# Sums over heads in a scan: squares as the moving operand, and spreading back by contractions over two rows

## The reference

```
kk = (k * k_k).reshape(b, L, 1, H, N)
kk = kk * rsqrt(sum(kk * kk, axis=-1, keepdims=True) + 1e-12)
... y = scan of both directions, summed ...
mean = mean(y, axis=-1, keepdims=True)
var = mean(square(y - mean), axis=-1, keepdims=True)
y = (y - mean) * rsqrt(var + GN_EPS) * ln_w + ln_b
bonus = sum(r * k_dir * r_k, axis=(2, 4))[..., None] * v
out = (y + bonus) * g
```

## Time and profile before

| | us |
|---|---|
| median of 3 runs | 2915.07 |
| lowest, highest | 2907.82, 2916.02 |
| the profiled execution | 2910.93 |
| its span | 2909.2 |
| PE busy | 2653.8 (91%) |
| PEld busy | 2209.6 (76%) |
| DVE busy | 1241.4 (43%) |
| ACT busy | 668.9 (23%) |
| POOL busy | 827.3 (28%) |

### The profile page before, as it was taken

How to read it: one execution, slowest core, us unless ns; L and a number is a source line. 1 busy time by engine, 2 the same in 40 slices (tenths; PEclk the granted TensorE clock), 3 DMA queues, 4 the chain that set the end, 5 groups by cost and what they waited for, 6 DMA issues and landing times. The chain is left out here.

```text
span 2909.2 us, 68114 instructions
## 1 busy us (share of the span) xinstructions
PE 2653.8 (91%) x29216; PEld 2209.6 (76%) x29216; DVE 1241.4 (43%) x2236; ACT 668.9 (23%) x1544; POOL 827.3 (28%) x644
## 2 busy tenths in 40 slices
PE   3987997997997999999999799596999999999997
PEld 2885456886886899998989655485888888888886
DVE  5003663551111444444444322565445544544545
ACT  3101551110001444444444211131011001101102
POOL 1222113332332233232333000543233233333324
PEclk9998998998998999999999999798999999999999
DMA  4111102101221000000000143432011111101113
GB/s 119 42 44 38 32 17 81 42 22 62 86 85 57 4 4 4 3 4 3 4 3 4 40 152 116 150 123 80 29 43 36 36 36 43 36 29 50 36 43 130
DMA packets 60191, 143.10 MB, mean 49 GB/s; under 512 B 12112, under 2 KB 31184, under 8 KB 59472
## 3 DMA queue, kind: packets, MB, share of 16 engines
q1 hardware_dynamic: 46176, 114.36, 12.0%
q10 hardware_dynamic: 10256, 12.49, 1.4%
q0 software_dynamic: 3552, 13.11, 1.1%
HBM read 108.48 MB, written 31.46 MB: 48 GB/s over the span
## 5 line engine op out<-in xcount | busy, mean ns | idle before, releaser
L1905 DVE TENSOR_TENSOR f<-f,ff_pd 128x512 f32<-128x512 f32 x320 | 214.2, 684 | 153.2 <-PE ff_pd L94 153.1
L1891 DVE TENSOR_TENSOR ff_sq<-ff_rl 128x512 f32<-128x512 f32 (+1 forms) x96 | 102.8, 1071 | 295.6 <-ACT ff_rl L1852 295.6
L1852 ACT ACTIVATE ff_rl<-ff_pu 128x512 f32<-128x512 f32 (+1 forms) x96 | 50.6, 527 | 759.0 <-PE ff_pu L94 759.0
L580 PE MATMUL sc_ps<-sc_xy,sc_q 64*64 64x64 f32 x3200 | 198.1, 221 | 0.0
L1053 DVE TENSOR_TENSOR sc_q<-sc_ps,sc_cs 128x128 f32<-128x128 f32 x400 | 113.6, 290 | 163.5 <-PE sc_ps L568 162.5
L577 PE MATMUL sc_ps<-sc_q,sc_xy 64*64 64x64 f32 x2560 | 170.6, 222 | 0.0
L568 PE MATMUL sc_ps<-sc_xy,sc_ai 64*64 64x64 f32 x3200 | 160.0, 223 | 1.4 <-ACT sc_xy L890 0.9
L890 ACT ACTIVATE sc_xy<-sc_ps 128x256 f32<-128x256 f32 x320 | 122.5, 383 | 160.3 <-PE sc_ps L580 159.7
L580 PEld LDWEIGHTS sc_ps<-sc_xy,sc_q 64*64 64x64 f32 x3200 | 156.1, 137 | 2.1 <-issue 1.0
L94 PE MATMUL ff_pu<-h2h,ff_wu0h 128*128 128x512 f32 (+1 forms) x384 | 136.8, 356 | 14.2 <-POOL ff_wu0l L1800 14.2
L429 POOL TENSOR_SCALAR sc_fac<-sc_icl,params,sc_k1a 128x512 f32<-128x512 f32 x20 | 15.3, 767 | 432.3 <-DVE sc_xy L955 414.5
(11 more groups left out here) (275 smaller groups left out, 7246.3 us busy)
## 6 DMA issues: line engine op xcount, KB each, us to landing
ff_wr<-in_w_up SPq DMA_DIRECT2D x32, 512.0 KB, 3.2
ff_wr<-in_w_down SPq DMA_DIRECT2D x32, 512.0 KB, 3.2
g_dram<-gp_g ACTq DMA_DIRECT2D x16, 640.0 KB, 2.9
mb_gate<-g_dram SPq DMA_DIRECT2D x8, 1280.0 KB, 8.9
gp_w<-in_w_in SPq DMA_DIRECT2D x16, 512.0 KB, 3.5
sp_w<-in_w_in SPq DMA_DIRECT2D x15, 512.0 KB, 3.5
n_x<-in_x SPq DMA_DIRECT2D x10, 512.0 KB, 3.6
m_dram<-mb_mo POOLq DMA_DIRECT2D x8, 640.0 KB, 8.9
```

The lines of the kernel that those rows point to most:

```text
L580: last = nc.tensor.matmul(y_out[g][rows, u, :], Q1[g][rows, u, :], XY[g][rows, 1, u, :], start=True, stop=True)
L1852: nc.scalar.activation(rl[u % 2][:, 0:tn], pu[b][:, 0:tn], ACT.Relu).then_inc(relu, 1)
L1891: nc.vector.tensor_tensor(sq[u % 2][:, 0:tn], rl[u % 2][:, 0:tn], rl[u % 2][:, 0:tn], ALU.mult).then_inc(squared, 1)
L1905: nc.vector.tensor_tensor(at, at, pd[d % 4][:, :], ALU.add).then_inc(added, 1)
```

## The change

- Two constants more: `by_heads`, 128x32, whose first two columns pick the channels of the two heads and whose other 30 are zero, and `by_row`, 128x128, which at rows 32p and 32p+1 (p = 0, 1, 2) has a one for each channel of the first or second head. The constants' load grows from 384 to 544 columns.
- `by_head` now has `by_heads` as weights and 512 tokens of the squares as moving operand, once for each of the three pieces, into partitions 32p to 32p+31 of one bank. The last piece takes the last 512 tokens, of which 256 are used.
- The square root and the inverse work on 96 partitions by 512 columns. The 1/64 of the variance is now the scale of the square root.
- `spread` and its POOL copies go, and with them two semaphores.
- `back` is one matmul for a piece: `by_row` at two rows as weights, the inverse norms at the same two rows as moving operand. Its wait is for the inverse.
- In front of the first step, the wait for the scan's constants moves ahead of `back`.

```diff
-        norms = [sb(f"sc_n{n}", [P, 2 * NT]) for n in range(2)]
+        norms = [sb(f"sc_n{n}", [P, 512]) for n in range(2)]
+        place = lambda p: slice(32 * p, 32 * p + 2)
+        full_piece = lambda p: slice(min(GROUPS[p][0], T - 512), min(GROUPS[p][0], T - 512) + 512)
+        in_piece = lambda p: slice(512 - GROUPS[p][1], 512)
+        placed = slice(0, 32 * NG)
...
-            def spread(ready, turn, norm, buf, done):
-                pool.wait_ge(ready, turn + 1)
-                nc.gpsimd.tensor_copy(buf[:, :].rearrange("p (n t) -> p n t", t=C),
-                                      norm[:, :].unsqueeze(2).to_broadcast([P, 2 * NT, C])).then_inc(done, 1)
...
-            def by_head(bank, sq, sums, done):
-                for n in range(NT):
-                    last = nc.tensor.matmul(ps[:, bank, 2 * n:2 * n + 2], sq[:, n * P:(n + 1) * P],
-                                            sums[:, 0:P:HD], start=True, stop=True)
-                last.then_inc(done, 1)
-
-            def back(bank, spread, p, done):
-                for m, n in enumerate(tiles_of(p)):
-                    last = nc.tensor.matmul(ps[:, bank, m * P:(m + 1) * P], spread[:, n * P:(n + 1) * P], ident,
+            def by_head(bank, sq, done):
+                for p in range(NG):
+                    last = nc.tensor.matmul(ps[32 * p:32 * p + 32, bank, :], by_heads, sq[:, full_piece(p)],
                                             start=True, stop=True)
                 last.then_inc(done, 1)
+
+            def back(bank, norm, p, done):
+                w = GROUPS[p][1]
+                nc.tensor.matmul(ps[:, bank, 0:w], by_row[place(p), :], norm[place(p), in_piece(p)], start=True, stop=True
+                                 ).then_inc(done, 1)
...
-                nc.scalar.activation(norms[1][:, :], ps[:, bank, 0:2 * NT], ACT.Sqrt,
-                                     bias=params[:, PM_EPS + 1:PM_EPS + 2]).then_inc(std_ready, 1)
+                nc.scalar.activation(norms[1][placed, :], ps[placed, bank, :], ACT.Sqrt, scale=1.0 / HD,
+                                     bias=params[placed, PM_EPS + 1:PM_EPS + 2]).then_inc(std_ready, 1)
...
-                nc.vector.reciprocal(norm[:, :], norm[:, :]).then_inc(done, 1)
+                nc.vector.reciprocal(norm[placed, :], norm[placed, :]).then_inc(done, 1)
...
-            pe.wait_ge(rnb_ready, 1)
+            pe.wait_ge(rn_ready, 1)
+            pe.wait_ge(cs_in, 16)
             for p in range(NG):
-                back(p, nrm, p, rnb_ps)
-            pe.wait_ge(cs_in, 16)
+                back(p, norms[0], p, rnb_ps)
```

More of the change, by code:

```diff
@@ L51 @@
 CN_ID, CN_ONES, CN_MEAN = 0, 128, 256
-CN_N = 384
+CN_HEADS, CN_ROWS = 384, 416
+CN_N = 544
 CS_G = BT
@@ L304, in _, with scan_mixer @@
             dve.wait_ge(shifted, E_SH + 2)
-def scan_mixer(nc, lora, params, cn_scan, ident, ones, mean, sT):
+def scan_mixer(nc, lora, params, cn_scan, ident, ones, mean, by_heads, by_row, sT):
     with ExitStack() as ctx:
@@ L363, in scan_mixer @@
             sem("p_ps"), sem("p"), sem("u_ps"), sem("u"), sem("s_ps"), sem("s"), sem("y_ps"), sem("y"))
[L364 to L367, removed]
+        sqk_ready, ss_ps, nrm_ready, rn_ready, rnb_ps, kk_ready = (
+            sem("sqk"), sem("ss_ps"), sem("nrm"), sem("rn"), sem("rnb_ps"), sem("kk"))
+        mean_ps, yc_ready, sqy_ready, var_ps, std_ready, rs_ready, rsb_ps, yn_ready = (
+            sem("mean_ps"), sem("yc"), sem("sqy"), sem("var_ps"), sem("std"), sem("rs"),
             sem("rsb_ps"), sem("yn"))
@@ L405, in turn_of @@
             return p if ct == CT - 1 else (0, 2, 1)[p]
-        def tiles_of(p):
-            return range(GROUPS[p][0] // P, (GROUPS[p][0] + GROUPS[p][1]) // P)
         @block.sync
@@ L480, in _ @@
             pool.wait_ge(scaled, 2)
-            spread(rn_ready, 0, norms[0], nrm, rnb_ready)
             prepare(0)
@@ L488, in _ @@
                     bonus_in(ct - 1)
[L489 to L492, removed]
                 if i == 3 and ct > 0:
@@ L672, in side @@
                     pe.wait_ge(sqy_ready, ct * NG)
-                    by_head(GRAM_BANK, std, mean, var_ps)
+                    by_head(GRAM_BANK, std, var_ps)
                 if i == 1 and ct + 1 < CT and l == 1:
@@ L676, in side @@
                     pe.wait_ge(sqk_ready, (ct + 2) * NG)
-                    by_head(TOK_BANK, nrm, ones, ss_ps)
+                    by_head(TOK_BANK, nrm, ss_ps)
                 if i == 1 and ct > 0 and l == 2:
@@ L686, in side @@
                     if p == 0:
-                        pe.wait_ge(rsb_ready, ct)
+                        pe.wait_ge(rs_ready, ct)
                     else:
                         pe.wait_ge(yn_ready, c * NG + 1)
-                    back(GRAM_BANK, std, p, rsb_ps)
+                    back(GRAM_BANK, norms[1], p, rsb_ps)
                 if i == 3 and ct + 1 < CT and p is not None:
                     if p == 0:
-                        pe.wait_ge(rnb_ready, ct + 2)
+                        pe.wait_ge(rn_ready, ct + 2)
                     else:
                         pe.wait_ge(kk_ready, (ct + 1) * NG + 1)
-                    back(GRAM_BANK, nrm, p, rnb_ps)
+                    back(GRAM_BANK, norms[0], p, rnb_ps)
                 if i == 4 and ct > 0 and p is not None:
@@ L712, in side_late @@
                 if i == 2 and ct > 0:
-                    back(TOK_BANK, std, 1, rsb_ps)
+                    back(TOK_BANK, norms[1], 1, rsb_ps)
                 if i == 3 and ct + 1 < CT:
-                    back(TOK_BANK, nrm, 1, rnb_ps)
+                    back(TOK_BANK, norms[0], 1, rnb_ps)
                 if i == 4 and ct > 0:
@@ L732, in _ @@
             pe.wait_ge(sqk_ready, NG)
-            by_head(GRAM_BANK, nrm, ones, ss_ps)
+            by_head(GRAM_BANK, nrm, ss_ps)
             lora_products(0, 0, 3)
             lora_products(0, 1, 3)
-            pe.wait_ge(rnb_ready, 1)
+            pe.wait_ge(rn_ready, 1)
+            pe.wait_ge(cs_in, 16)
             for p in range(NG):
-                back(p, nrm, p, rnb_ps)
-            pe.wait_ge(cs_in, 16)
+                back(p, norms[0], p, rnb_ps)
             pe.wait_ge(nrm_ready, 1)
@@ L806, in _ @@
             pe.wait_ge(sqy_ready, CT * NG)
-            by_head(STATE_BANK, std, mean, var_ps)
-            pe.wait_ge(rsb_ready, CT)
+            by_head(STATE_BANK, std, var_ps)
+            pe.wait_ge(rs_ready, CT)
             for p in range(NG):
-                back(p, std, p, rsb_ps)
+                back(p, norms[1], p, rsb_ps)
             pe.wait_ge(bv_ready, CT * NG)
@@ L1938, in encoder @@
         params, cn = sb("params", [P, PM_N]), sb("cn", [P, CN_N])
-        ident, ones, mean = (cn[:, c:c + P] for c in (CN_ID, CN_ONES, CN_MEAN))
+        ident, ones, mean, by_row = (cn[:, c:c + P] for c in (CN_ID, CN_ONES, CN_MEAN, CN_ROWS))
+        by_heads = cn[:, CN_HEADS:CN_HEADS + 32]
         with nc.semaphore("const_in") as const_in, nc.Block() as block:
@@ L1955, in encoder @@
                 gate_projection(nc, a["w_in"], params, H, g_dram)
-            scan_mixer(nc, a["lora"], params, a["cs"], ident, ones, mean, sT)
+            scan_mixer(nc, a["lora"], params, a["cs"], ident, ones, mean, by_heads, by_row, sT)
             merge_branches(nc, a["w_proj"], g_dram, oa_dram, sT[:, 0:CT, :], m_dram)
@@ L1970, in host_constants @@
     heads = np.kron(np.eye(2, dtype=np.float32), np.ones((HD, HD), np.float32))
-    cn = np.concatenate([eye, heads, heads / HD], axis=1)
+    by_heads, by_row = np.zeros((P, 32), np.float32), np.zeros((P, P), np.float32)
+    by_heads[:, 0:2] = heads[:, 0:P:HD]
+    for p in range(NG):
+        by_row[32 * p:32 * p + 2, :] = heads[0:P:HD, :]
+    cn = np.concatenate([eye, heads, heads / HD, by_heads, by_row], axis=1)
     reset = np.ones(BT, np.float32)
```

5 lines of the change are left out of this document (2 added, 3 removed).

## The result

| | before | after |
|---|---|---|
| median of 12 runs, us | 2911.34 | 2917.81 |
| lowest, highest, us | 2907.09, 2916.05 | 2913.70, 2921.56 |
| ratio, with its 95% interval | | 1.0022 [1.0014, 1.0031] |
| the profiled execution, us | 2910.93 | 2917.69 |
| its span, us | 2909.2 | 2915.9 |

The change costs 6.5 us where a gain of 1.5 was forecast. The time lies in the stated range and within 0.3% of before, but the interval excludes no change: the sign was wrong. The forecast of 2914 us stood on three runs of before, median 2915.07; twelve give 2911.34, so it is the difference between the kernels that counts here.

A forecast was written before the change was run, and what follows sets the result against it. PE was taken to bound the scan, busy 198 of 200 us; +2.6 us inside the scan and -3.4, -1.0, +0.3 outside gave -1.5 on the median 2915.1, about 2914 us, range 2902 to 2928.

The forecast's parts named there:

- six by_head: Squares' sums on PE inside the scan: 1.0 us each instead of 2.3, column tiles side by side; -7.9 us.
- stalls in the four steps, at full clock: Second steps, ct 0 to 3: join 3 waits behind the reciprocals and PE for it; 3.1, 4.7, 4.7, 1.6: +14.1 us.
- half clock behind by_head, gone: Five half-clock stretches of PE in the scan, each after a by_head, taken as gone: -6.5 us.
- half clock behind the stalls: Four new half-clock stretches of PE expected behind the new idle stretches of 3 to 5 us: +4.2 us.
- back in the scan: Two passes of 512 a piece, 1.0 us instead of 1.1; six turns at some 0.2 us: -1.3 us.
- beginning: Start of the scan, at half clock: shorter by_head and back bring POOL's first product forward from 928.0 to 924.6: -3.4 us.
- end: End of the scan: shorter by_head and back, copy gone, longer root and reciprocal; 5.75 us against 6.8: -1.0 us.
- rival D: A by_head of 32 weight columns leaves the clock at half, 6.5 us not won: about 2920 us; chance 0.09.
- Rivals A: Slower: the reciprocal repeats for each element and costs 5.1 us; +14 us, 2928; chance 0.18.
- B: Faster: the reciprocal costs like any other 128x512 operation, 0.7 us; about 12 us lower, 2901; chance 0.10.
- Rival E: Half of the 14.1 us of stall finds cover as queues regroup behind the first late joins; 7 us less, 2907; chance 0.05.
- rival C: The three column tiles of by_head do not run side by side: +9.9 us inside the scan, 2928; chance 0.06.

The follow-up runs named there:

- filled kernel: The changed kernel with unread pairs of 64x64 matmuls in PE's idle stretches of the four side-work steps: 2913.35 us, ratio to before 1.0000.
- the second execution: Both kernels, unchanged, run and profiled once more: after 2918.68 us, before 2913.44 us.
- the kernel in parts: The changed kernel with each of the six reciprocals inside the scan cut into eight of 96x64, each behind a join: 2899.07 us, ratio to before 0.9948.
- the kernel with the cheap operation: The changed kernel with its eight 96x512 reciprocals replaced by an ordinary operation of that shape, norms left out: 2898.45 us, ratio to before 0.9950.

## Why the prediction was wrong, point by point

**The step that failed is the clock, and in it the half clock behind the stalls.** It stood in the sum at +4.2 us and measured +8.1. Put beside the forecast, in us:

| | forecast | measured or worked out |
|---|---|---|
| six by_head | -7.9 | -8.0 |
| stalls in the four steps, at full clock | +14.1 | +15.7 |
| half clock behind by_head, gone | -6.5 | -6.7 |
| half clock behind the stalls | +4.2 | +8.1 |
| the clock, net | -2.3 | +1.4 |
| back in the scan | -1.3 | -0.4 |
| the first step, a pause of before's | 0 | -0.8 |
| the scan from its first to its last step | +2.6 | +8.0 |
| beginning | -3.4 | -3.7 |
| end | -1.0 | -0.2 |
| larger constants | +0.3 | +0.3 |
| sum | -1.5 | +4.4 |

The terms go back to runs. The filled kernel is after with nothing at half clock in the four steps: 161.6 us, so +8.1. The same for before has no run of its own and is worked out: ct 0 ran at full clock (35.5), ct 3 did in the second execution (37.8), and ct 1 and 2 would be the 38.0 of the kernel in parts at ct 2 and full clock, plus two by_head of 1.33 us more, less 0.4 for the shorter wait for the root, 40.3 each. That is 153.9 in all, so before's five stretches cost 6.7 us. Between 153.9 and 161.6 lie the by_head and the stalls, which gives the stalls 15.7. The second pair of executions has 4.2 us of half clock in before's three stretches and 6.0 in after's five, net +1.8: the sign is the same.

The sum of +4.4 us is that of one pair of profiles, with its attention left out. The medians say +6.5, by the interval 4.1 to 9.0, and the second pair of profiles +5.1 in the scan stage. So some 4.5 to 5.5 us are located, and the remaining one or two may lie within the measurement or be the clock's own variation; that is open.

Of the clock's two halves the first was right: before has its five stretches behind by_head, after has none directly behind one, they were worth 6.7 us, and rival D, in which the light weights leave the clock halved, is out. But they are worth that in one execution; in the next they were three and 4.2 us. The second half was mis-sized in number and in price. Behind the stalls stand seven stretches and not four: at ct 0 and ct 3 two follow each other, and it is the wait for the root, 1.9 us, that the first at ct 1 and at ct 3 follow, a wait I had not counted among the idle stretches that cost the clock. And 4.2 us for four is 1.05 each, with no reason given, where I had put one behind by_head at 1.5; the single one at ct 2 cost 44.24 - 42.79 = 1.45. The bounds I gave, -6.5 and +4, held the value. The sign of what I took within them did not.

PE goes from 2.4 to 1.2 GHz (granted 0.50) near the end of an idle stretch or soon behind it, so that the next work is slow: at 996.6 with PE's next product at 997.26, at 1167.2 behind one at 1167.00, at 1174.0 behind 1173.65, at 1355.0 behind 1354.87, at 1529.0 behind 1527.71. The Trainium skill, page "TensorE: Matmul & The Clock Gate", section "HAM oscillation — how this bites in real kernels", tells of a kernel whose short bursts of matmuls between waits start at the lower clock each time. By that rule each long stall of this change is paid again in part, and the filled kernel agrees, 8.1 us.

**The reciprocal, right.** 3.2 us were forecast from the slope between 1 and 20 elements, and it took

```profile
L949 DVE RECIPROCAL sc_n<-sc_n 96x512 f32<-96x512 f32 x8 | 26.5, 3335 | 15.7 <-ACT sc_n L842 8.9 <-ACT sc_n L837 6.8
```

which is (3335 - 164) / 511 = 6.2 ns an element. Rivals A (5.1 us) and B (0.7 us) are out. The estimate from the Trainium skill, page "VectorE: DVE Perf Modes", section "First, the fixed hardware budget", was 4.4 us, from a repeat of 8 at one cycle each. The measurement decides, and it lies a quarter under that.

**Where it falls, right.** Stalls stand at the four places named. By place: in front of join 3's product PE waits 2.8, 2.9, 4.5 and 0.65 us at ct 0 to 3, where 3.1, 4.7, 4.7 and 1.6 were forecast, and for the root 1.9 us instead of 0.9 to 1.5. At ct 1 the half-clock stretch behind the root's wait makes PE's own work before the product longer and so hides 1.6 us of the stall: in the second execution of after, which has no such stretch there, PE waits 4.47 us at ct 1 as at ct 2. At ct 3 it is the same: in the filled kernel, at full clock, the product starts 1.4 us later in the step than in the kernel with the cheap operation. So at full clock the join costs 2.8, 4.5, 4.5 and 1.4, 13.2 against 14.1. What the forecast left out of its sum is the longer wait for the root, +0.4 us four times (at ct 0 it is PE's wait for ACT's copy behind the root), although it had the longer root at +0.35. The rest of the 15.7 is in no wait of its own. Rival E, in which half of it finds cover, is out by the sum.

**by_head, right.** Six passes in 1.06 us at full clock, the next product 0.99 after the start (1.0 forecast), and 1.93 at half clock. Column tiles of 128 rows by 32 columns run side by side, so rival C is out.

**back, too high.** A piece of 512 holds PE for 1.05 us (1201.92 to 1202.97) where the 8 passes had held it for 1.09. The estimate of 0.2 a turn was a difference of two roundings; 0.4 us in six turns is what the steps show.

**The beginning and the end.** From the stage's start to POOL's first product 12.4 us instead of 16.1, -3.7 (-3.4 forecast). The stage started 3.7 us later in this execution, nearly all of it behind the attention, and the first product of the scan's first step came at 949.86 against 949.91. At the end nothing of that size is won. Rows after, where the earlier trace rows stand before:

```profile
1658.15 0.68 ACT L842 ACTIVATE sc_n<-sc_ps,params 96x512 f32<-96x512 f32 x1 [0.63 <-PE sc_ps L640]
1658.87 3.35 DVE L949 RECIPROCAL sc_n<-sc_n 96x512 f32<-96x512 f32 x1 [1.14 <-ACT sc_n L842]
1662.27 2.08 PE L646 MATMUL sc_ps<-sc_n,cn 2*128 2x512 f32 x6 [4.18 <-DVE sc_n L949]
1664.38 1.80 DVE L960 SCALAR_TENSOR_TENSOR sc_y<-sc_y,params,sc_ps 128x512 f32<-128x512 f32 x3 [2.16 <-PE sc_ps L646]
```

Reciprocal 3.35 instead of 3.1, back 2.08 at the half clock that the 4.2 us of idle time bring, and all three of DVE's products behind it: 7.3 us from the reciprocal's start to the last product's end, where 6.7 was forecast and before had 6.8. The last step and its end together are 0.2 us shorter.

**POOL.** As forecast, the copies' going changes nothing inside the scan; nothing waited for them there.

**The chances.** A time within 0.3% of before was given 0.60 and is what came, but a band of 8.7 us to either side is wide beside a forecast of -1.5, and that the time fell into it says little for the sum. The error of the sum is 8.0 us by the medians. The profiles show 5.9 of it: 3.7 in the clock, 1.6 in the stalls, 0.9 in back and 0.8 at the end, less 1.1 elsewhere. The other 2.1 are not located.

## What to carry to other kernels

A layout that turns 20 columns into 512 multiplies every operation whose time goes by the free size: before folding a norm into fewer matmuls, count the reciprocal at 6.2 ns a column and ask which short operation stands behind it in its engine's queue. If the engine has a wait of 0.4 us in each round, cut the long operation into parts of about that size and put one into each round: the same work that cost 21 us in one piece cost nothing measurable in eight. Where PE is the bound, count an idle stretch more than once, here 8.1 us of half clock on 17.8 us of waits, and give nothing for the clock on the gain side before a second profile of the same kernel has shown that its stretches are there again: here the second had three of five.

## What the runs showed of the hardware that was not expected

- PE's clock halves behind some idle stretches of 1.9 us (at 1167.2 in after, behind 1.87 us), and stays at 1.2 GHz for 3.4 us or 6.8. At ct 2 of the same execution, and at ct 1 of the next, the same 1.87 us had no half clock behind it.
- Unread matmuls in the idle time made the kernel 6.4 us faster: the clock stayed at 2.4 GHz in the four steps, 1.00 where it had been 0.92 to 0.96.
- Two executions of one kernel differ by 4 us in the attention and by two of five half-clock stretches in the scan, with the same instructions: a difference between two profiles of that size is not yet one between two kernels.
- A reciprocal of 96x512 takes 3.29 to 3.35 us, of a norm as of a tile of ones, and one of 96x64 takes 0.54.
